# GpSimd subtracts each weight panel's high part in two pieces of 1024 columns, not four of 512

## What is computed

```python
def reference(x, ...):
    # first block
    h = rms_norm(x) * (1 + scale1) + shift1
    proj = h @ w_in                                    # q, k, v, z, mla_q, gates ...
    o_a = gated_delta_rule(q_a, k_a, v_a, g_a, beta_a) @ w_out_dn
    o_b = mla_attention(mla_q, mla_ckv, mla_kr, ...) @ w_out_mla
    x = x + gate1 * ((sigmoid(gate_dn) * o_a + sigmoid(gate_mla) * o_b) @ w_o)
    up = h2 @ ffn_w_up                                 # D_FF = 2816, two halves
    x = x + gate2 * ((gelu(conv(a_path)) * v_path) @ ffn_w_down)
    # second block
    proj = rmsnorm(x) @ w_in_2
    y_a = rwkv7_mix(...) @ w_o_rwkv;  y_b = dsa_attention(...) @ w_o_att
    h = x + (g_a * y_a + g_b * y_b) @ w_out
    z_gate, z_up = split(rmsnorm(h) @ w_ffn_in)        # 2816 columns each
    return rmsnorm(h + (silu(z_gate) * z_up) @ w_ffn_out)
```

## Time and profile before

| | before |
|---|---|
| median of 3 runs | 2029.47 us (2026.11 to 2029.76) |
| the profiled execution's own time | 2029.86 us |
| its span, first to last instruction | 2028.1 us |
| PE busy | 1972.6 us, 97% |
| DVE busy | 918.6 us, 45% |
| ACT busy | 823.1 us, 41% |
| GpSimd busy | 992.2 us, 49% (of it the 588 subtractions: 782.6 us) |
| granted clock of PE, mean | 0.995 of full speed |

### The profile page before, as it was taken

How to read it: one execution, slowest core, us unless ns; L and a number is a source line. 1 busy time by engine, 2 the same in 40 slices (tenths; PEclk the granted TensorE clock), 3 DMA queues, 4 the chain that set the end, 5 groups by cost and what they waited for, 6 DMA issues and landing times.

```text
span 2028.1 us, 26209 instructions
## 1 busy us (share of the span) xinstructions
PE 1972.6 (97%) x10110; PEld 1605.9 (79%) x10110; DVE 918.6 (45%) x1502; ACT 823.1 (41%) x1098; POOL 992.2 (49%) x767
## 2 busy tenths in 40 slices
PE   6999999999999999999999999999999999999997
PEld 3787987867778878888888678977877788888886
DVE  2678648967331324222101886459954521112101
ACT  4567234346561333232222755254336542222321
POOL 3737634645215555565655572043542356555662
PEclk9999999999999999999999999999999999999999
DMA  7312025531112322222223220033221222222222
GB/s 290 105 63 84 22 86 232 207 110 63 38 46 104 131 98 84 104 85 103 104 104 135 104 84 22 2 103 108 97 83 63 109 99 95 92 104 94 97 101 83
DMA packets 30827, 199.59 MB, mean 98 GB/s; under 512 B 5488, under 2 KB 7664, under 8 KB 9712
## 3 DMA queue, kind: packets, MB, share of 16 engines
q1 hardware_dynamic: 30704, 197.92, 27.0%
HBM read 188.99 MB, written 4.19 MB: 95 GB/s over the span
## 4 chain that ended last, share of the span: by engine, by line
PE 88%; DVE 6%; ACT 3%; DMA 1%; issue 1%; POOL 0%; SPq 0%; DVEq 0%; ACTq 0%; POOLq 0%
PE ps L451 23%; PE ps L452 23%; PE ps L453 23%; PE ps L527 2%; PE ps L469 1%; PE ps L470 1%; DMA ar<-ada_dram 1%; PE ps L903 1%; PE ps L557 1%; PE ps L492 1%; PE ps L890 1%; PE ps L667 1%; PE ps L1226 1%; DVE ps L2039 1%; PE ps L1234 1%
## 5 line engine op out<-in xcount | busy, mean ns | idle before, releaser
L2669 POOL TENSOR_TENSOR WL<-raw,WH 128x512 fp32r<-128x512 f32 x588 | 782.6, 1331 | 852.1 <-ACT WH L1383 809.7
L451 PE MATMUL ps<-hH,WH 128*128 128x512 f32 x1560 | 619.6, 397 | 2.8 <-ACT ar L1447 1.6
L453 PE MATMUL ps<-hH,WL 128*128 128x512 f32 x1560 | 608.3, 390 | 0.0
L452 PE MATMUL ps<-arR,WH 128*128 128x512 f32 x1352 | 526.0, 389 | 0.0
L1383 ACT CAST WH<-raw 128x2048 fp32r<-128x2048 f32 x147 | 280.9, 1911 | 472.8 <-DMA raw<-panels_dram 471.7
L451 PEld LDWEIGHTS ps<-hH,WH 128*128 128x128 f32 x1560 | 293.5, 188 | 74.8 <-issue 13.7
L453 PEld LDWEIGHTS ps<-hH,WL 128*128 128x128 f32 x1560 | 293.4, 188 | 62.2
L452 PE MATMUL ps<-xL,WH 128*128 128x512 f32 x792 | 309.6, 391 | 0.0
L452 PEld LDWEIGHTS ps<-arR,WH 128*128 128x128 f32 x1352 | 253.8, 188 | 52.9 <-issue 0.5
L451 PE MATMUL ps<-arR,WH 128*128 128x512 f32 x584 | 227.9, 390 | 0.0
L453 PE MATMUL ps<-arR,WL 128*128 128x512 f32 x584 | 227.2, 389 | 0.0
(11 more groups left out here) (408 smaller groups left out, 2401.1 us busy)
## 6 DMA issues: line engine op xcount, KB each, us to landing
raw<-panels_dram SPq DMA_DIRECT2D x145, 1024.0 KB, 4.8
ar<-ada_dram SPq DMA_DIRECT2D x12, 2048.0 KB, 11.2
xT<-xT_dram SPq DMA_DIRECT2D x2, 2048.0 KB, 8.7
out_dram<-xT SPq DMA_DIRECT2D x8, 512.0 KB, 2.8
ar<-ar SPq DMA_DIRECT2D x12, 256.0 KB, 7.1
xT<-out_dram SPq DMA_DIRECT2D x1, 2048.0 KB, 9.2
wide<-wide_dram SPq DMA_DIRECT2D x1, 1024.0 KB, 4.8
ar<-ar SPq DMA_DIRECT2D x8, 128.0 KB, 3.9
```

The costliest lines, as they stand in the source:

```text
L451: mm(out, lhs[0], rhs[0], start=first, stop=False)
L452: mm(out, lhs[0], rhs[1], start=False, stop=False)
L453: return mm(out, lhs[1], rhs[0], start=False, stop=final)
L2669: ins = tt(WL[:, n % SLOTS, c], raw[:, n % SLOTS, c], WH[:, n % SLOTS, c].bitcast(F32), ALU.subtract)
```

## The change

The loop over a panel's columns in GpSimd's `split` has two turns of 1024 columns where it had four of 512. WL gets the same numbers, the link between the pieces and the semaphore behind the last one stay.

```diff
-                    for q in range(4):
-                        c = slice(q * PANEL // 4, (q + 1) * PANEL // 4)
+                    for q in range(2):
+                        c = slice(q * PANEL // 2, (q + 1) * PANEL // 2)
                         ins = tt(WL[:, n % SLOTS, c], raw[:, n % SLOTS, c], WH[:, n % SLOTS, c].bitcast(F32), ALU.subtract)
-                        if q < 3:
+                        if q < 1:
                             link(ins)
                         else:
                             link(ins, panel_low, n + 1)
```

## The result

The changed kernel takes 2042.14 us by the median of 4 runs (2039.94 to 2046.63), the kernel before 2028.66 (4 runs, 2026.11 to 2029.76): a ratio of 1.0069, interval 1.0057 to 1.0081, so slower by some 12 to 16 us. The forecast was 2033.5 and its range ended at 2036.8.

A forecast was written before the change was run, and what follows sets the result against it. PE, busy 1972.6 of 2028.1 us, was taken as the bound, with longer DVE holds as the cost. 3.2 + 0.3 + 0.5 = +4.0 us on the median of 2029.47 gave 2033.5 us, range 2028.6 to 2036.8.

The forecast's parts named there:

- The piece: GpSimd's subtraction of 1024 columns: forecast 2.48 us, from 1.29 us for 512 and 98 ns fixed.
- side remark: An alternative estimate of 2.36 us for 1024 columns, which would take about 0.7 us off the sum.
- What GpSimd owns: PE's idle time that ends on GpSimd: one wait of 0.3 us for a low part, left out of the sum.
- The hold: A DVE instruction blocked by a GpSimd piece: about 2.15 us extra in place of 0.96.
- rival (b): The shared resource is split while both engines run, so DVE's times stay: -0.3 to 0 us, 2029.3 us; chance 0.07.
- Items 1 to 3: First attention, panels at 468.81, 481.70 and 491.46 us: longer DVE holds cost PE 3.2 us.
- Item 1: First attention, panel at 468.81 us: four held DVE instructions, +0.5 us; +0.1 counted with GpSimd's earlier end.
- Rival (a): First attention's chain realigns, so its holds partly or wholly go: 0 to +2 us, 2029.5 to 2031.5; chance 0.22.
- Item 4: Second block's decays, panel at 1152.06 us: two held DVE instructions, +2.4 us, 2.1 covered, +0.3 reaches PE.
- Item 5: Rope before the second block's index scores, panel at 1363.94 us: four held DVE instructions, +0.5 us.
- Item 6: Everywhere else, chiefly 300 to 420 us: some ten panels, 5 us in all, covered by 10.41 us idle; nothing counted.
- rival (d): Slower still if cover is thinner or shifted panels meet later attention units: +6 to +9 us, 2035.5 to 2038.5; chance 0.14.

The follow-up runs named there:

- e1: Changed kernel with panels 15 to 25 (the gates) back in four pieces, all others in two: 2037.0 us, ratio 1.0036.
- e4: Kernel before with only panels 26 to 29 (first attention) in two pieces, all others in four: 2034.6 us, ratio 1.0024.
- e9: Kernel before with two pieces only in panels 82 to 146, four in all earlier ones: 2031.4 us, ratio 1.0018.
- e10: The changed kernel run again unaltered, for a second trace: 2040.0 us, ratio 1.0057 to the kernel before.
- e13: Kernel before with the first DVE operation of ada products 8 (L2115) written 16 times and not once: 2035.5 us, ratio 1.0035.
- e17: Kernel before with the first DVE operation of ada products 7 (L2115) written 16 times: 2042.7 us, ratio 1.0074.
- e8: Kernel before with one piece of 2048 columns in every panel: 2053.8 us, ratio 1.0122.
- e2: Kernel before with only panels 15 to 25 (the gates) in two pieces, all others in four: 2033.8 us, ratio 1.0023.
- e5: Changed kernel with the SyncE load of ada columns 8 moved behind panel (mq, 1)'s load: 2038.1 us, ratio 1.0049 to the kernel before.
- e3: Changed kernel with panels 15 to 29 (gates and first attention) in four pieces, the rest in two: 2031.4 us, ratio 1.0015.
- e12: Kernel before with eight pieces in panels 26 to 29 (first attention), four elsewhere: 2031.0 us, ratio 1.0008.
- e15: Kernel before with two pieces in panels 0 to 14 and 30 to 81, eight in 26 to 29, four elsewhere: 2030.0 us, ratio 0.9999.
- e7: Kernel before with eight pieces of 256 columns in every panel: 2035.4 us, ratio 1.0036.

## Why the prediction was wrong

**The piece** was a term mis-sized. 2.48 us was forecast, 2.40 measured (739, 1292, 2397 and 4609 ns for 256, 512, 1024 and 2048 columns: 186 ns fixed and 2.16 ns a column). I had taken the fixed part, 98 ns, from the clearing of tiles. The side remark's estimate of 2.36 from the Trainium skill, "GPSIMD Engine Reference", section 3.1, was nearer.

**What GpSimd owns.** The list of waits also had 1.5 us in two waits for its masks (L725 <- L2735), which the prediction passed over. They are the same in all kernels.

**The hold** was right: 2.79 - 0.75 = 2.04 us where 0.96 was; 2.15 was forecast. That the engines are held for whole instructions and not for a share of the port is shown from 256 to 2048 columns, and rival (b) is out.

**Items 1 to 3**, the attention: 3.2 us forecast on PE, 2.3 measured, in three kernels (after, e1, e4). The rows came as written, and DVE's step of 2.7 us in items 2 and 3 is near the 3.1 forecast. Item 1's 0.6 isn't there on DVE (6.25 us late at 441 us, 6.06 at 478), and PE wasn't as tight ahead of L557 as "all of it is PE's" had it. Rival (a) is out.

**Item 4**: the wait of L527 grew from 3.2 to 3.4 us, forecast +0.3. **Item 5**: +0.5 us forecast, none found; L1204's wait is 2.3 us in all and was 2.6.

**Item 6** is the step that failed. Its amount for a panel (+0.5 us in 3.8) was right where I could read it out. Its cover was not. I looked for the end of DVE's row of work, found 10.41 us of idle time there, and called the stretch covered. But DVE's instructions in it are waited for one by one on the way: PE uses each product, SyncE waits for `ada_used`, and a panel stands behind it. The slack there was 3.94 us, and DVE ran 7 us late around 360 us. That cost 3.7 us of wait and 3.3 us of clock, where the sum had nothing. The text had the mechanism in rival (d), "if the cover of item 6 ... is thinner", at 0.14, with 2035.5 to 2038.5.

**What no case had.** First, the last softmax chain, where one hold makes PE wait 1.1 us more, and up to 1.0 us in the units ahead of it (e9, e10). I had called everything but five places covered without looking at it. Second, the clock: I let each us of wait cost one us. The runs say that PE's time rises by more than its waits: 3.3 us behind L613's and 4.0 behind the last L557's in both traces of the changed kernel. Without the clock the result would be 7 to 8 us above the kernel before, and not the forecast's 4.0: the gates' 3.7 and the last attention's 1.1 to 2.2 are what it didn't have, and the attention's 2.3 is less than it had.

**What stays open.** At the gates the clock's cost is caused by the wait: in all 20 profiles, the 7 with a wait of L613 from 1.2 us up have the fall there, and the 13 with 0.3 us or none don't; e13 and e17 make it with four pieces on GpSimd. By PE's rows the fall costs 3.3 us in both traces of the changed kernel and in e13, 2.9 in e17, 2.4 in e8 and 1.7 in e2 and e5. Elsewhere it isn't settled. Here are two gaps of PE around 1317 us that are the same in both kernels, 1.03 and 0.83 us; first the kernel before, then e3:

```profile
1315.00:1320.00 5.00, 3.97 (x41) 1.00 0.01 3
1320.00:1325.00 5.00, 4.17 (x14) 1.00 0.31 105
```

```profile
1315.00:1320.00 5.00, 3.97 (x24) 0.68 0.01 3
1320.00:1325.00 5.00, 4.17 (x23) 0.50 0.19 66
```

PE is busy for the same time up to 1320 us, but e3 gets through 24 matmuls in it and the kernel before through 41. What PE did ahead of the gap is the same to 0.01 us in both, the clock behind it isn't, and what follows is some 4 us later. This fall stands in 9 of the 20 profiles, with two pieces and with four. So I can't say that two pieces cause it, nor why the kernel before, at 10.5 us lost, seems to have it seldom (one of its executions is traced), and e12 and e15, whose waits are shorter, lose 2 to 3 us more. The same holds for 1595 us, where the fall stands behind the waits of 2.5 us in five of nine profiles, and not in e1, e3, e8 and e9; e7 has it behind one of 1.9 us.

## What to carry to other kernels

A resource that two engines hold for whole instructions couples the size of one engine's pieces to every chain of the other. Where the held engine's work has no gaps, the sum of the holds hardly changes with the size; what changes is how many of them fall ahead of a signal. Look for cover at each signal that leaves the held engine (a matmul, a DMA queue with something behind it), not at the idle time at the end of its row. And where PE is 97% busy, a wait of a few us can cost as much again by the clock behind it.

## What the runs showed of the hardware

The seven waits of PE at L613, 1.2 to 10.8 us long, each had the clock at its lower level behind them, at a cost of 1.7 to 3.3 us. Gaps of 1.03 and 0.83 us around 1317 us had it in 9 of 20 profiles, at some 4 us. The Trainium skill, "TensorE: Matmul & The Clock Gate", Part 1, says that the number of slow matmuls at a kernel's start varies from run to run of one kernel; the two traces of the changed kernel agree, with a clock of 0.94 and 0.69 from 25 to 30 us, and the falls in mid-kernel vary at the same gaps too (1317 us, in one of the two).

An instruction of 2 columns (L2599, 0.17 us) can be held for 1.3 us. DVE's L2073, which reads PSUM, took its usual 0.42 us at 1570.42 us in the kernel before, in the midst of a panel.

A load of 1 MB took 10.13 us behind one of 2 MB in the same queue, against 4.8 us by the median of the panel loads.
